# Expert weights in transfers of one k-tile: 512 KB instead of 1 MB, 24 ring slots instead of 12

## What is computed

```python
def expert_choice_ffn(h, router, w_gate, w_up, w_down):
    cap = CAPACITY_FACTOR * t // N_EXPERTS            # 64 latent tokens, 32 context tokens
    aff = softmax(h @ router)
    gate, idx = top_k(swapaxes(aff, 1, 2), cap)       # every expert takes its own tokens
    xs = h[bidx, idx]
    hid = silu(xs @ w_gate) * (xs @ w_up)
    y = (hid @ w_down) * gate[..., None]
    return zeros_like(h).at[bidx, idx].add(y)
```

## Time and profile before

| | us |
|---|---|
| median of 3 runs | 3123.28 |
| lowest and highest of the 3 | 3120.75 and 3128.16 |
| the profiled execution, device time | 3124.46 |
| its span, first to last instruction | 3122.7 |
| mean granted TensorE clock, share of full speed | 0.915 |
| SP issues of expert weights (L988) | 384 of 1024 KB |
| median from issue to landing of one of them | 21.8 |

### The profile page before, as it was taken

How to read it: one execution, slowest core, us unless ns; L and a number is a source line. 1 busy time by engine, 2 the same in 40 slices (tenths; PEclk the granted TensorE clock), 3 DMA queues, 4 the chain that set the end, 5 groups by cost and what they waited for, 6 DMA issues and landing times. The chain is left out here.

```text
span 3122.7 us, 33638 instructions
## 1 busy us (share of the span) xinstructions
PE 2579.2 (83%) x13966; PEld 1540.1 (49%) x13966; DVE 1148.7 (37%) x1937; ACT 457.5 (15%) x932; POOL 242.8 (8%) x208
## 2 busy tenths in 40 slices
PE   4999879299999994999787687777748766799999
PEld 2585665144444432578435222222237534688888
DVE  3635674500000004227675300000053666534551
ACT  2101441200000002000241100000010221111000
POOL 1000001001111102002001000000021200100000
PEclk8999879699999996999898799999969866899999
DMA  6331312689999964435002899999822100122221
GB/s 241 142 122 66 93 61 95 253 343 388 389 396 396 390 271 140 148 126 151 26 0 109 323 397 396 402 403 394 347 95 96 45 12 1 68 81 88 98 81 58
DMA packets 97959, 603.60 MB, mean 193 GB/s; under 512 B 12408, under 2 KB 15816, under 8 KB 32656
## 3 DMA queue, kind: packets, MB, share of 16 engines
q1 hardware_dynamic: 85024, 572.96, 47.1%
q0 software_dynamic: 11632, 26.39, 3.8%
q10 hardware_dynamic: 1152, 2.10, 0.2%
HBM read 574.03 MB, written 23.18 MB: 191 GB/s over the span
## 5 line engine op out<-in xcount | busy, mean ns | idle before, releaser
L1021 PE MATMUL moe_psg<-moe_ring,moe_xs 128*64 128x512 f32 x1024 | 253.6, 636 | 41.4 <-DMA moe_ring<-in_experts 39.2
L1021 PE MATMUL moe_psd<-moe_ring,moe_hid_t 128*64 128x512 f32 x1024 | 237.3, 602 | 30.1 <-DMA moe_ring<-in_experts 28.5
L1183 DVE TENSOR_SCALAR moe_y_l<-moe_psd,moe_gates 128x512 f32<-128x512 f32 x32 | 24.0, 751 | 644.9 <-PE moe_psh L1035 331.5
L1021 PE MATMUL moe_psu<-moe_ring,moe_xs 128*64 128x512 f32 x1024 | 235.8, 599 | 30.3 <-DMA moe_ring<-in_experts 30.1
L1021 PEld LDWEIGHTS moe_psg<-moe_ring,moe_xs 128*64 128x64 f32 x1024 | 72.6, 144 | 192.3 <-issue 163.1
L1021 PEld LDWEIGHTS moe_psd<-moe_ring,moe_hid_t 128*64 128x64 f32 x1024 | 68.7, 137 | 190.0 <-issue 129.3
L1175 DVE TENSOR_TENSOR moe_hid_l<-moe_silu_l,moe_psu 128x512 f32<-128x512 f32 x32 | 22.0, 688 | 365.8 <-PE moe_psgu L1035 189.8
L1021 PEld LDWEIGHTS moe_psu<-moe_ring,moe_xs 128*64 128x64 f32 x1024 | 67.1, 136 | 177.1 <-issue 110.9
L1084 POOL DMA_INDIRECT acc_lat<-moe_y_l,moe_rows_id x32 | 50.1, 1564 | 915.3 <-DVE moe_y_c L1185 464.6
L1035 PE MATMUL moe_psgu<-moe_ring,moe_xs 128*32 128x256 f32 x2048 | 117.1, 380 | 0.0
L1035 PEld LDWEIGHTS moe_psgu<-moe_ring,moe_xs 128*32 128x32 f32 x2048 | 63.3, 110 | 64.4 <-issue 26.0
(11 more groups left out here) (645 smaller groups left out, 4278.0 us busy)
## 6 DMA issues: line engine op xcount, KB each, us to landing
moe_ring<-in_experts SPq DMA_DIRECT2D x384, 1024.0 KB, 21.8
feed_f_slots<-in_ffn_gate SPq DMA_DIRECT2D x11, 1024.0 KB, 4.9
feed_f_slots<-in_ffn_up SPq DMA_DIRECT2D x11, 1024.0 KB, 4.8
feed_f_slots<-in_ffn_down SPq DMA_DIRECT2D x8, 1408.0 KB, 6.0
mod_ada_w<-in_ada_w SPq DMA_DIRECT2D x2, 4096.0 KB, 13.4
qk_ada_w<-in_ada_w SPq DMA_DIRECT2D x8, 1024.0 KB, 4.8
gate_rows<-in_ada_w SPq DMA_DIRECT2D x8, 1024.0 KB, 5.4
mout_ada_w<-in_ada_w SPq DMA_DIRECT2D x8, 1024.0 KB, 4.8
```

The costliest lines, as they stand in the source:

```text
L1021: mm = pe.matmul(ps_lat[part][64 * half:64 * half + 64, :], lhs, ring[:, n % SLOTS, m, half * HALF:(half + 1) * HALF], start=(k == 0), sto ...
L1183: ins = dve.tensor_scalar(y_l[:], ps_lat[DOWN][:], gates[:, 0, e, :], None, ALU.mult)
```

## The change

One transfer is now one k-tile of one matrix (512 KB, 4 KB per partition) and not two. The ring has 24 slots of half the size, so it still holds 12 MB in the same memory. There are 24 `landed` semaphores in place of 12, a wait for each k-tile in `lat_pass`, and `w_used` is raised once per k-tile. All counts (`first_chunk`, `used_up`, `source`) are in k-tiles. The number of transfers of a layer goes from 192 to 384, of `first_expert` from 12 to 24. The matmuls, their order and operands stay. The host lays the weights out so that each k-tile is one contiguous block.

```diff
--- before.py
+++ after.py
@@ -969,16 +969,16 @@
         if e + 1 < EXPERTS:
             order.append((e + 1, GATE))
         order.append((e, DOWN))
-    first_chunk = {what: 4 * n for n, what in enumerate(order)}
-    source = [e * 12 + 4 * part + c for e, part in order for c in range(4)]
-    used_up = lambda e, part: first_chunk[e, part] + 4
+    first_chunk = {what: KT * n for n, what in enumerate(order)}
+    source = [(3 * e + part) * KT + k for e, part in order for k in range(KT)]
+    used_up = lambda e, part: first_chunk[e, part] + KT
 
     with ExitStack() as ctx:
         sb = lambda n, s, t=F32: ctx.enter_context(nc.sbuf_tensor(f"{name}_{n}", s, t))
         rows_id = sb("rows_id", [P, 3, EXPERTS], U32)
         gates = sb("gates", [P, 2, EXPERTS, 1])
-        SLOTS = 12
-        ring = sb("ring", [P, SLOTS, 2, D])
+        SLOTS = 24
+        ring = sb("ring", [P, SLOTS, D])
         sig = Signals(nc, name)
         landed = [sig[f"w_landed_{s}"] for s in range(SLOTS)]
 
@@ -1011,30 +1011,26 @@
 
             def lat_pass(pe, e, part, chunks):
 
-                for c in chunks:
-                    n = first_chunk[e, part] + c
+                for k in chunks:
+                    n = first_chunk[e, part] + k
                     pe.wait_ge(landed[n % SLOTS], 16 * (n // SLOTS + 1))
-                    for m in range(2):
-                        k = 2 * c + m
-                        for half in range(2):
-                            lhs = xs[:, e % 2, k, 0:64] if part != DOWN else hid_t[:, k % 4, 64 * (k // 4):64 * (k // 4) + 64]
-                            mm = pe.matmul(ps_lat[part][64 * half:64 * half + 64, :], lhs,
-                                           ring[:, n % SLOTS, m, half * HALF:(half + 1) * HALF],
-                                           start=(k == 0), stop=(k == KT - 1))
+                    for half in range(2):
+                        lhs = xs[:, e % 2, k, 0:64] if part != DOWN else hid_t[:, k % 4, 64 * (k // 4):64 * (k // 4) + 64]
+                        mm = pe.matmul(ps_lat[part][64 * half:64 * half + 64, :], lhs,
+                                       ring[:, n % SLOTS, half * HALF:(half + 1) * HALF],
+                                       start=(k == 0), stop=(k == KT - 1))
                     if not both:
                         mm.then_inc(sig["w_used"], 1)
 
             def ctx_pass(pe, e, part):
 
-                for c in range(4):
-                    n = first_chunk[e, part] + c
-                    for m in range(2):
-                        k = 2 * c + m
-                        for q in range(4):
-                            lhs = xs[:, e % 2, k, 64:96] if part != DOWN else hid_t[:, 4 + k % 2, 32 * (k // 2):32 * (k // 2) + 32]
-                            mm = pe.matmul(ps_ctx[part][32 * q:32 * q + 32], lhs,
-                                           ring[:, n % SLOTS, m, q * QUARTER:(q + 1) * QUARTER],
-                                           start=(k == 0), stop=(k == KT - 1))
+                for k in range(KT):
+                    n = first_chunk[e, part] + k
+                    for q in range(4):
+                        lhs = xs[:, e % 2, k, 64:96] if part != DOWN else hid_t[:, 4 + k % 2, 32 * (k // 2):32 * (k // 2) + 32]
+                        mm = pe.matmul(ps_ctx[part][32 * q:32 * q + 32], lhs,
+                                       ring[:, n % SLOTS, q * QUARTER:(q + 1) * QUARTER],
+                                       start=(k == 0), stop=(k == KT - 1))
                     mm.then_inc(sig["w_used"], 1)
 
             def turn_rows(pe, e):
@@ -1098,7 +1094,7 @@
                 def _(pe):
                     turn_rows(pe, 0)
                     pe.wait_ge(sig["xs"], 1)
-                    lat_pass(pe, 0, GATE, range(4))
+                    lat_pass(pe, 0, GATE, range(KT))
                     if both:
                         ctx_pass(pe, 0, GATE)
                     for e in range(EXPERTS):
@@ -1107,7 +1103,7 @@
                             turn_rows(pe, e + 1)
                         if e >= 1:
                             pe.wait_ge(sig["hid"], e)
-                        lat_pass(pe, e, UP, range(4))
+                        lat_pass(pe, e, UP, range(KT))
                         if both:
 
                             pe.wait_ge(sig["silu"], (e + 1) * len(streams))
@@ -1116,9 +1112,9 @@
 
                             pe.wait_ge(sig["xs"], e + 2)
                             pe.wait_ge(sig["silu"], (e + 1) * len(streams))
-                            lat_pass(pe, e + 1, GATE, range(2))
+                            lat_pass(pe, e + 1, GATE, range(KT // 2))
                             turn_hidden(pe, e)
-                            lat_pass(pe, e + 1, GATE, range(2, 4))
+                            lat_pass(pe, e + 1, GATE, range(KT // 2, KT))
                             if both:
                                 ctx_pass(pe, e + 1, GATE)
                         else:
@@ -1126,7 +1122,7 @@
                         pe.wait_ge(sig["hid_t"], e + 1)
                         if e >= 1:
                             pe.wait_ge(sig["y"], e)
-                        lat_pass(pe, e, DOWN, range(4))
+                        lat_pass(pe, e, DOWN, range(KT))
                         if both:
                             ctx_pass(pe, e, DOWN)
 
@@ -2649,7 +2645,7 @@
     for layer in range(DEPTH):
 
         w = np.stack([i[n][layer] for n in ("moe_w_gate", "moe_w_up", "moe_w_down")], 1)
-        a[f"experts{layer}"] = w.reshape(EXPERTS * 12, 2, P, D).transpose(0, 2, 1, 3)
+        a[f"experts{layer}"] = w.reshape(EXPERTS * 3 * KT, P, D)
 
     a["ada_w"] = i["ada_w"].reshape(DEPTH, KT, P, N_MOD, D).transpose(0, 3, 2, 1, 4)
     a["router"] = i["moe_router"].reshape(DEPTH, KT, P, EXPERTS).transpose(0, 2, 1, 3)
```

## The result

The changed kernel is slower, as forecast, and by more: a median of 3141.3 us over 6 runs beside 3122.2 us for 6 runs of the kernel before. The ratio is 1.0055, with a 95% interval of 1.0038 to 1.0072. The forecast was +10.4 us, 3133.7 in a range of 3121 to 3143; by the ratio +17 us came (0.0055 x 3122). The profiled execution is the fastest of the six: 3132.3 us, span 3130.5. So I don't compare the spans, but stretches of the two traces that begin and end with the same instruction.

The account below looks back on a forecast made before the run. Layer 0 was taken as bound by TensorE (33.8 us per expert), layer 1 by transfers (32.9). The terms 2.8 + 9.3 - 1.7 = +10.4 us gave a median of 3133.7 us, range 3121 to 3143.

Parts of the forecast that it names:

- The held prefetch: Norm blocks before the experts: SP, blocked issuing 24 loads, reaches the barrier late; +2.8 us layer 0, +9.3 us layer 1.
- The step of 2.1 us: SP's issues into a full queue: a blocked issue tries again in steps of 2.1 us, the uncertainty of each delay.
- The cover by the stores: End of layer 1's route block: stores land about as before, covering 1.7 us of the 11.0 us delay, leaving +9.3.
- Ten transfers, whatever their size: SP's queue: holds about ten transfers of any size, so half as large transfers leave half as many bytes queued.
- Transfer size: Weight loads of both expert stages: 4 KB instead of 8 KB rows leave the rate unchanged, 0; bad end 5.8 us.
- Rival two: Delay as forecast, plus slower reads with 4 KB rows in layer 1: +5.8 us, 3139.5 us in all; chance 0.12.
- Layer 0 hides the slower loads: Layer 0 experts: TensorE sets the pace at 33.8 us per expert, so slower loads would cost nothing there.
- The finer hand-back: Layer 1's first refill and last chunk: ring space returned in halves gains 0.8 and 0.9 us, together -1.7 us.
- Waits on TensorE: Expert matmuls in `lat_pass`: four more waits per matrix don't show, 0.
- clearing barriers: Semaphore clears between stages: six before and six after, all where every engine waits; 0, a microsecond either way.

Follow-up runs that it names:

- the prefetch in two blocks: The changed kernel with 12 of the 24 first loads issued in the norm block and 12 at the start of the route block; 1.0018 of the kernel before.

## Why the prediction was right in direction and short in size

**The held prefetch: right in place, a little large, and its limit misread.** The barrier of layer 1 was forecast 11.0 us late and was 9.0, that of layer 0 2.8 and was 1.9. SP's last issue of layer 1 ended 19.6 us after the first, when 13 of the 24 had landed, and not at 22.2 with 14. The step of 2.1 us, taken for a retry, fits a wait for transfers to drain: with 512 KB most blocked issues take 1.1 us, with 1 MB 2.1 and more. The cover by the stores held: in layer 1 9.0 late at the barrier, 7.5 at the first weight matmul, where 1.7 of cover was forecast. Of layer 0's delay nothing is left at the read-back. Its router matmuls ran 5.19 us in place of 6.17, at a granted clock of 0.70 and not 0.58, and its last DOWN pass 7.09 in place of 8.74, at 1.00 and not 0.88; the forecast had no term for the clock. Both came again in the second trace of the changed kernel; the prefetch in two blocks had 0.89 in that pass. What in the change would cause it is not shown. "Ten transfers, whatever their size" was wrong as a rule, and came near because the stores and the new loads both have nine packets per transfer like the old loads. The kernel with twelve loads of 4 KB rows shows it.

**Transfer size: the step that failed.** I took 0 for the rate, since the stores of 512 KB and 4 KB rows move 419 GB/s. They write; reads with 4 KB rows move 411. The nearest read row, 414, was in my hand and became a rival. By it layer 1 should have lost 5.8 us; it lost 33.50 - 32.89 = 0.61 us per expert, 9.8 for 16. It is the largest part of what was missing: with 9.8 added and the barriers at their measured size at the first weight matmuls, 0.6 + 7.5 + 9.8 - 1.7 is 16.2 us. Rival two was the case that came, at a chance of 0.12. That the forecast of 10.4 us had the right direction rests on the held barrier; that it came within 7 us is in part luck, since its barriers were 4 us too large (12.1 against 8.1) and hid part of the missing term.

**Layer 0 hides the slower loads: right.** 33.80 us per expert before and after, and no wait for weights (window 640:1165).

**The finer hand-back: right at the start, its worth not shown.** The first refill came 2.0 us after the first matmul instead of 3.7, 1.7 sooner as forecast. The whole is 0.3 to 3.5 us between single traces, for the forecast 1.7.

**Waits on TensorE and clearing barriers at 0: the waits right, the barriers open.** The 33.80 us hold for the waits. There are six clears before and after, as counted, and three have only moved. But outside the expert layers the three traces with 24 `landed` semaphores are 6 to 8 us shorter than that of the kernel before, and no other is; no run tells the cause.

**Size of transfer or size of row.** 1 MB transfers with 4 KB rows lose as much as 512 KB transfers with them (33.46 us and 33.46 us per expert with equal waits), so no fixed cost per transfer was paid here. The rule of the Trainium skill ("DMA: Bandwidth & Descriptors", section "Rules for kernel authors"), at least 1 MiB per DMA, pointed the right way; by the runs it is the row that set the rate, which the rule does not name as the cause. The 2.0 us that the prediction took from the Trainium skill, same page, section "Anatomy of one DMA", stand there for transfers issued by GpSimd; these are issued by SP.

## What to carry to other kernels

When a load is cut in smaller pieces, look at what becomes of its contiguous rows, and price them with a row of the trace that goes in the same direction: here rows of 4, 8 and 16 KB that lie side by side read at 411, 417 and 429 GB/s. Count the packets that a prefetch puts in front of the issuing engine; here it stood still at 85 to 119 per DMA engine, and with it every barrier that it had to reach. Where fine hand-back is thought to pay, at the first refill and at the last chunk, it can be had there alone. And before a sum of stretches is compared with a difference of medians, look whether the rest of the two traces is equal: here it was 6 us off.

## What the runs showed of the hardware that I had not expected

- Reads with longer rows are faster beyond 8 KB: 429 GB/s with 16 KB (a packet took 0.613 us, one of 8 KB 0.315). Rows of 4 KB that lie 8 KB apart read at 397. And stores with 4 KB rows (419 to 422) are not slow as reads are (410 and 411).
- The 4 KB rows need not be many transfers to block SP: twelve took 17.1 us, while the twelve with 8 KB rows took 7.9.
- A load of 64 partitions instead of 128, with the same rows, runs at 220 GB/s with all DMA engines shown as busy: each packet takes twice as long (0.60 us). Why was not tried.
